# A decoder layer with streamed weights: x and inner tiles at a pitch of 1152 bytes, weight tails written over the raw chunks

## The reference: what is computed

```python
x = x + 0.5 * swiglu(rms_norm(x, g1), w_gate1, w_up1, w_down1)    # 2048 -> 5632 -> 2048
h = rms_norm(x, g2);  p = h @ w_in                                  # 2048 -> 6400
# p: attention q,k,v (8 heads of 64) | RWKV-7 r,k,v and three low-rank inputs | gated conv u,B,C
x = x + concat(attention, rwkv7, conv) @ w_out                      # 2048 -> 2048
x = x + 0.5 * swiglu(rms_norm(x, g3), w_gate2, w_up2, w_down2)
```

## Time and profile before

| | us |
|---|---|
| median of three runs | 2331.7 |
| lowest and highest run | 2325.49, 2332.32 |
| span of the profiled execution | 2324.0 |
| busy: PE, DVE, ScalarE, POOL | 2237.5, 1220.7, 884.0, 209.7 |
| FFN 1 gate/up, then down | from 33 to 553, to 809 |
| w_in with its side work | to 1158 |
| RWKV | to 1434 |
| w_out | to 1530 |
| FFN 2 gate/up, then down | to 2048, to the end |

### The profile page before, as it was taken

How to read it: one execution, slowest core, us unless ns; L and a number is a source line. 1 busy time by engine, 2 the same in 40 slices (tenths; PEclk the granted TensorE clock), 3 DMA queues, 4 the chain that set the end, 5 groups by cost and what they waited for, 6 DMA issues and landing times.

```text
span 2324.0 us, 44718 instructions
## 1 busy us (share of the span) xinstructions
PE 2237.5 (96%) x18348; PEld 2208.0 (95%) x18348; DVE 1220.7 (53%) x1279; ACT 884.0 (38%) x1011; POOL 209.7 (9%) x173
## 2 busy tenths in 40 slices
PE   6999999999999999999967998999999999999997
PEld 5999999999999999999947988999999999999997
DVE  5555555554454456698454244555555555544442
ACT  4444444343444344343142141444444444333332
POOL 2000000000000000242029301000000000000000
PEclk9999999999999999999765587999999999999999
DMA  5555555555555565778410001555555555555553
GB/s 160 181 179 180 176 179 178 181 180 172 181 180 184 180 192 156 221 212 266 141 35 1 28 29 45 180 179 179 175 179 180 179 176 178 180 177 188 180 173 109
DMA packets 359028, 373.43 MB, mean 161 GB/s; under 512 B 13329, under 2 KB 351797, under 8 KB 358742
## 3 DMA queue, kind: packets, MB, share of 16 engines
q1 hardware_dynamic: 349280, 348.17, 48.0%
q0 software_dynamic: 5920, 17.48, 3.0%
q10 hardware_dynamic: 3742, 6.52, 0.9%
HBM read 366.82 MB, written 5.32 MB: 160 GB/s over the span
## 4 chain that ended last, share of the span: by engine, by line
PE 91%; DVE 5%; DMA 2%; ACT 1%; issue 1%; POOL 0%; ACTq 0%; SPq 0%; POOLq 0%; DVEq 0%
PE ps L298 27%; PE ps L297 27%; PE ps L299 26%; PE ps L1578 2%; PE ps L1572 2%; DMA raw<-in_w_in_dram 2%; DVE wL L285 1%; PE ps L1584 1%; PE ps L1056 1%; PE ps L1391 1%; DVE xL L331 0%; PE ps L1619 0%; PE ps L1610 0%; ACT wH L279 0%; DMA vrowa<-in_rwkv_mu_dram 0%
## 5 line engine op out<-in xcount | busy, mean ns | idle before, releaser
L285 DVE TENSOR_TENSOR wL<-raw,wH 128x1024 fp32r<-128x1024 f32 (+1 forms) x676 | 828.6, 1231 | 881.1 <-ACT wH L279 880.5
L279 ACT ACTIVATE wH<-raw 128x1024 fp32r<-128x1024 f32 (+1 forms) x676 | 701.3, 1040 | 1030.2 <-PE ps L299 956.4
L297 PE MATMUL ps<-xH,wH 128*128 128x264 f32 x3616 | 1036.2, 287 | 12.3 <-DVE wL L285 12.3
L298 PE MATMUL ps<-xL,wH 128*128 128x264 f32 x3616 | 1035.6, 286 | 0.0
L299 PE MATMUL ps<-xH,wL 128*128 128x264 f32 x3616 | 1033.6, 286 | 0.0
L297 PEld LDWEIGHTS ps<-xH,wH 128*128 128x128 f32 x3616 | 687.6, 190 | 14.3 <-issue 13.6
L299 PEld LDWEIGHTS ps<-xH,wL 128*128 128x128 f32 x3616 | 685.4, 190 | 0.0
L298 PEld LDWEIGHTS ps<-xL,wH 128*128 128x128 f32 x3616 | 684.9, 189 | 0.2
L298 PE MATMUL ps<-hL,wH 128*128 128x264 f32 x1408 | 400.4, 284 | 0.0
L299 PE MATMUL ps<-hH,wL 128*128 128x264 f32 x1408 | 399.5, 284 | 0.0
L297 PE MATMUL ps<-hH,wH 128*128 128x264 f32 x1408 | 398.8, 283 | 0.0
(11 more groups left out here) (332 smaller groups left out, 1481.2 us busy)
## 6 DMA issues: line engine op xcount, KB each, us to landing
raw<-in_ffn_w_gate_dram SPq DMA_DIRECT2D x176, 512.0 KB, 3.5
raw<-in_ffn_w_up_dram SPq DMA_DIRECT2D x176, 512.0 KB, 3.5
raw<-in_ffn_w_down_dram SPq DMA_DIRECT2D x128, 512.0 KB, 3.5
raw<-in_w_in_dram SPq DMA_DIRECT2D x100, 512.0 KB, 4.9
raw<-in_ffn_w_down_dram SPq DMA_DIRECT2D x64, 384.0 KB, 3.0
raw<-in_w_out_dram SPq DMA_DIRECT2D x32, 512.0 KB, 3.8
kb<-in_cache_swa_k_dram POOLq DMA_DIRECT2D x24, 256.0 KB, 6.7
vb<-in_cache_swa_v_dram ACTq DMA_DIRECT2D x24, 256.0 KB, 4.9
```

The source lines that it names most:

```text
L279: nc.scalar.activation(wH[:, k % RING, 0:nk, :], raw[:, k % RING, 0:nk, :], ACT.Copy).then_inc(S("head_made"), 1)
L285: nc.vector.tensor_tensor(wL[:, k % RING, 0:nk, :], raw[:, k % RING, 0:nk, :], wH[:, k % RING, 0:nk, :].bitcast(F32), ALU.subtract).then_i ...
L297: nc.tensor.matmul(out, wH[:, k % RING, q, cols], vH[:, k0 + q, :], start=a, stop=False)
L298: nc.tensor.matmul(out, wH[:, k % RING, q, cols], vL[:, k0 + q, :], start=False, stop=False)
```

## The change

The tiles of xH, xL, hH and hL are placed at a pitch of NP = 288 numbers, 1152 bytes; each tensor is allocated with that pitch and then cut to its first N = 264 columns, so all code that reads it is as before. wL is placed where raw is: a chunk's tail is written over the raw data it is made from. The tail's slot is now read by the PE, so `load` waits for `chunk_used` instead of `tail_made`, and `head` no longer needs to wait for it itself. There are four chunks on the way at most. S2 moves to the new place of wL, so the first load of w_out waits for `sample_y`. The 16 KB that come free hold the longer tiles; xr, M0 and all that hangs on them move.

```diff
+NP = 288
...
     raw = at("raw", [P, RING, CK, CW], F32, 0)
     wH = at("wH", [P, RING, CK, CW], F32R, 16384)
-    wL = at("wL", [P, RING, CK, CW], F32R, 32768)
-    xr = at("xr", [P, KT, N], F32, 49152)
-    M0 = 66048
-    hH = at("hH", [P, FT, N], F32R, M0)
-    hL = at("hL", [P, FT, N], F32R, M0 + 46464)
-    xH = at("xH", [P, KT, N], F32R, M0 + 92928)
-    xL = at("xL", [P, KT, N], F32R, M0 + 109824)
-    E0 = M0 + 126720
+    wL = at("wL", [P, RING, CK, CW], F32R, 0)
+    xr = at("xr", [P, KT, N], F32, 32768)
+    M0 = 49664
+    HB, XB = FT * NP * 4, KT * NP * 4
+    hH = at("hH", [P, FT, NP], F32R, M0)[:, :, 0:N]
+    hL = at("hL", [P, FT, NP], F32R, M0 + HB)[:, :, 0:N]
+    xH = at("xH", [P, KT, NP], F32R, M0 + 2 * HB)[:, :, 0:N]
+    xL = at("xL", [P, KT, NP], F32R, M0 + 2 * HB + XB)[:, :, 0:N]
+    E0 = M0 + 2 * HB + 2 * XB
...
-    yst = at("yst", [P, 2, 2, CW], F32, M0 + 92928)
-    yss = at("yss", [NB, 2, CW], F32, M0 + 92928 + 4096)
-    yf = at("yf", [P, 2, 2, N], F32, M0 + 92928 + 6144)
+    yst = at("yst", [P, 2, 2, CW], F32, M0 + 2 * HB)
+    yss = at("yss", [NB, 2, CW], F32, M0 + 2 * HB + 4096)
+    yf = at("yf", [P, 2, 2, N], F32, M0 + 2 * HB + 6144)
...
-    S2 = at("S2", [96, C, C], F32, 32768)
+    S2 = at("S2", [96, C, C], F32, 0)
...
     def load(sp, view, k0, nk, pair, first, per, i, k, fresh=False):
         if not fresh:
-            sp.wait_ge(S("tail_made"), number(first, per, i, k) - RING + 1)
+            sp.wait_ge(S("chunk_used"), number(first, per, i, k) - RING + 1)
...
     def head(act, nk, first, per, i, k, fresh=False):
         act.wait_ge(S(f"landed{k % RING}"), i * (16 * (per // RING)) + 16 * (first // RING + k // RING + 1))
-        if not fresh:
-            act.wait_ge(S("chunk_used"), number(first, per, i, k) - RING + 1)
...
     def sp_out(sp):
+        sp.wait_ge(S("sample_y"), 2)
         with sp.Fori(0, KT // 2) as i:
```

## The result

The changed kernel takes 2359.7 us in the median of 3 runs (2353.2 to 2362.6), the kernel before 2331.7. The ratio on record is 1.0128, 95% interval 1.0106 to 1.015: slower by 28 to 30 us, where 2320 was forecast. The profiled execution of the changed kernel took 2362.6 us with a span of 2360.9; the span of the profiled execution before is 2324.0. That makes 36.9 us to be explained between these two spans, some 9 more than between the medians: the profile of before is of a fast execution, that of after is of the slowest of the three.

The account below looks back on a forecast made before the run. TensorE was taken as the bound: number of matmuls times their start-to-start step. Span 2324.0 - 27 (pitch) + 16 (ring) = 2313 us; with 7.7 us carried over, 2320.7, say 2320 us; range 2302 to 2356.

Parts of the forecast that it names:

- pitch, gate/up: Gate/up: 8448 matmuls step 120.2 ns instead of 122.4 with aligned tiles, 18.6 us gained.
- pitch, down: Down projection: 4224 matmuls step 120.2 ns instead of 121.3, 4.6 us gained.
- pitch, w_in: w_in projection: 1800 PE-paced matmuls gain 2.2 ns each, 4.0 us; nothing where DVE paces.
- ring, x entries and gate/up: Stage entries needing finished x: 2 us lost at FFN 2, under 1 at w_in; gate/up itself loses nothing.
- ring, down: Down projection: 7 pair ends lose some 0.4 us each, 3 us, within 0 to 16.
- a choice near it: Padded tiles: mean step taken as 120.2 ns, near the 120.0 floor of an aligned tile.
- Rival (a): Whole kernel: the pitch does nothing and the ring alone counts, 2348 us; chance 0.18.
- rival (c): Padded tiles: half the pitch gain, odd and even multiples of 128 behaving differently, 2334 us; chance 0.11.
- the w_in term: w_in: loads waiting for the PE cost 2 + 3 + 6 = 11 us, bounds 7 and 41.
- rival (b): w_in: the ring is dear beside k and v cache loads, 41 us and some 9 in down, 2355 us; chance 0.12.
- the cover of 2.8 us in steady state: Gate/up: tails still finish 2.8 us before the PE needs them, so the ring costs nothing there.
- The wait at the x entry of FFN 2: FFN 2 entry: tails of x ready at 1540.7, wanted by the PE at 1538.4, 2 us lost.

Follow-up runs that it names:

- e4: The changed kernel with the xH and xL tiles at a pitch of 1280 bytes; 2333.1 us, one run.
- e6: The changed kernel with GpSimd waiting for one sequence's three key loads before issuing the next three; 2347.0 us, ratio 1.0085.
- e7: The changed kernel with x tiles at 1280 bytes, h back at 1056, and six raw slots in w_in; 2321.4 us, ratio 0.996.
- e3: The changed kernel with pitch 1056 and eight raw slots, tails still written over the raw chunks; 2324.6 us, ratio 0.998.
- e13: The changed kernel with xL moved up by 128 bytes; 2353.7 us, one run.
- e14: The changed kernel with the whole x region moved up by 256 bytes; 2346.4 us, one run.
- e1: The changed kernel with the pitch back at 1056 bytes, leaving the single ring alone; 2361.2 us, ratio 1.0134.
- e2: The kernel before with only xL moved up by 128 bytes; 2317.9 us, ratio 0.9951.
- e5: The kernel before with hL and xH moved up by 128 bytes and xL by 192; 2327.0 us, one run.
- e11: The kernel of e4 with the x region moved up by 256 bytes; 2355.4 us, one run.
- e9: The kernel of e7 with the x region moved up by 256 bytes; 2316.9 us, ratio 0.994.
- e12: The kernel of e9 with GpSimd waiting for each sequence's three key loads before the next three; 2317.9 us, ratio 0.9952.
- e8: The changed kernel profiled once more with no edit; 2370.1 us, one run.

## Why the prediction was wrong

The terms of the sum, against the 36.9 us between the two profiled spans (us, plus is slower). The forecast was -11 between spans, so 48 us separate the two; the rows below account for all but some 0.4 of them:

```
                                     forecast  measured  from
pitch, gate/up                         -18.6     -6.9    8448 x (122.49 - 121.67)
pitch, down                             -4.6     +1.2    4224 x (121.67 - 121.39)
pitch, w_in                             -4.0     -0.6    1800 x (122.18 - 121.86)
ring, w_in                             +11       +24.8   373.2 - 349.0 + 0.6
ring, x entries and gate/up             +2       +4.7    (517.6 + 518.5) - (520.0 + 518.3) + 6.9
ring, down                              +3       +1.3    +0.6 and +1.9, less 1.2
RWKV                                     0      +12.0    287.9 - 275.9
```

**The step that failed first is "a choice near it": the mean of 120.2 ns.** 120.0 exists as a steady mean (e4 runs at it), but the mean at this pitch was 121.67. The prediction had written that neighbouring tiles would still differ by 128 bytes modulo 256 and gave that 0.2 ns; it is 1.67. Of the 27 us promised, 6.3 came. Down was even made slower, since at 1056, with hH and hL 128 bytes apart, it had a better pattern (121.39) than the padded one. The evidence was two tiles of one pair, read as if a tile's own address made its step. The trace of before speaks against that reading: averaged over gate/up its tiles repeat in eights, and tile 4, which starts on a multiple of 128 like tile 0, steps 123.8 ns where tile 0 has 119.9. In the changed kernel tiles 1 and 3 begin alike modulo 256 and step 122.0 and 120.0, and in e6 they change places at unchanged addresses. Rival (a) had named what comes before a tile as a reason, and rival (c) a partial gain, at twice this size (-14). This term is 21 us of the 48.

**The second step that failed is the w_in term, +11, which measured 24.8.** Its sum took landings as some 4 us and held the long ones to be queued behind bursts of their own ring. But those near the cache loads are long because of the cache loads: chunk 323 took 11.98 us, with the load before it out 2.9 us earlier and landed in 4. The term then allowed 3.7 us a pair at most, taking the lost cover as one landing; it is 19.6 - 10.3 = 9.3 us, the whole second ring. Pair 12 lost 9.3 us: 6.3 of PE idling, 2.4 of a chunk at the lower clock, the rest small. e6 shows the burst's part by spreading it, e7 and e3 show that depth covers it. That is rival (b), with 25 us instead of its 41. That (b)'s total, 2355, lies near the measured 2359.7 is luck: it kept the 27 us of pitch, of which 6.3 came, and had nothing in RWKV.

**Right:** the cover of 2.8 us in steady state (2.7), that heads wait for DMA, that landings in gate/up stay covered (after the first chunk no PE wait for a weight tail there), the down stages (3 forecast, about 1.3), and the w_out loads behind sample_y (w_out is 95.6 us in both). The wait at the x entry of FFN 2 was right as well (2 forecast, 1.9 measured), but not its price. Before, w_in had no such wait; now it has the same 1.9 us, where under 1 was forecast. And in FFN 2 the PE ran some 15 matmuls behind the wait at 0.22 us a step, the lower clock, so that this entry cost some 3.7 us. The 7.7 us that the sum carried over from span to median lie between executions: in every run on record the time is only 1.6 to 1.8 us over its span.

**Not foreseen:** the sum had nothing for RWKV, and it measured 12 us. Shown is the lower clock in its last third, that it came in both profiles of the changed kernel, and that e6, e13 and e14, with ring and pitch unchanged, are without it. Other kernels have 281, so three levels occur (276, 281, 288 to 291). What picks one isn't known. Without it this change would stand at some +25 us between spans, which is what its own two parts give. e1, the ring alone, stands at +35 with RWKV at 276, of which 28.6 are w_in; so w_in under one and the same ring differs by 4 us from kernel to kernel.

## What to carry to other kernels

Count the depth of a ring from the issue of the load to the use, and hold it against the longest burst of other transfers, not against the median landing: with slots freed by the last engine instead of the first, four were too few for a 2.4 MB burst of another queue; six nearly held, eight did. Freeing memory by writing in place is fine if the slots saved go back into depth. And two tiles of one trace aren't a mean: before an address pattern is priced, average over a whole period of it in a steady stretch, and try moving a base by 128 bytes before paying for padding; here that brought 0.5% for 128 bytes, while the padding took 11.5 of the 16 KB that the ring gave up.

## What the runs showed of the hardware

- The start-to-start time of 264-column matmuls with fp32r operands in an unbroken stream lay at 120.0, 121.3 to 121.4, 121.67, 122.2 to 122.5 or 122.78 ns, at the full clock, steady over thousands of matmuls. Which values a kernel shows changes with the bases and pitch of the moving tiles (e2, e4, e5, e11, e13), and one program can show two of them (e9 and e12: 121.3 and 120.0; e8: 122.78 and 121.67). No such mean came under 120.0, though single tiles did (118.5 for one tile of eight in e2).
- 1280 bytes of pitch gave a flat 120.0 at all tiles in e4 and a flat 121.3 in e7 and e11; 1152 gave 120.0 at one tile in four.
- A 512 KB load took 3.5 us in the median of gate/up and 11.98 us when issued into nine 256 KB loads of another queue; in the kernel before the longest beside them took 14.8.
- DVE's tail operation took 3.57 us instead of 1.23 while GpSimd multiplied a 128x1536 tile, 970.73 to 974.15. Every tail over 1.6 us in the traces of before (7, up to 5.15 us) and after (8, up to 4.94) overlapped such a product.
- After 6.3 us of idling the PE started its next 24 matmuls over 5.23 us instead of 2.83, at 1.2 GHz instead of 2.4. In RWKV, where the PE is busy 231 of 276 us, the same instructions took 276, 281 or 288 to 291 us; the granted clock of the last third was 0.74 at 276 and 0.65 at 288.
